# Reordering the output-projection stage of a one-core hybrid encoder layer: variance before half a weight remainder, three row blocks of one column half first, MLP turns earlier

## The reference, cut to what matters

```
u = rms_norm(h, g_pre_mix)
proj = u @ w_in                                   # 1024 x 2304
o_a, o_b, o_c = stick_breaking(...), rg_lru(...) * gelu(...), sliding_window(...)
mixed = concat(rms_norm(o_a, ga), rms_norm(o_b, gb), rms_norm(o_c, gc))
y = mixed @ w_out                                 # 1024 x 1024
h = h + rms_norm(y, g_post_mix)
u = rms_norm(h, g_pre_mlp)
f = square(relu(u @ w_ff_in))                     # 1024 x 4096
h = h + rms_norm(f @ w_ff_out, g_post_mlp)
```

## Time and profile before

| | |
|---|---|
| median of 3 runs | 1014.74 us (1014.56 to 1014.86) |
| profiled execution, its own time | 1013.88 us |
| profiled execution, span | 1012.0 us |
| PE busy | 999.9 us (99% of the span) |
| DVE busy | 778.8 us (77%) |
| ACT busy | 577.4 us (57%) |
| POOL busy | 79.2 us (8%) |
| granted TensorE clock, mean | 0.999 |

### The profile page before, as it was taken

How to read it: one execution, slowest core, us unless ns; L and a number is a source line. 1 busy time by engine, 2 the same in 40 slices (tenths; PEclk the granted TensorE clock), 3 DMA queues, 4 the chain that set the end, 5 groups by cost and what they waited for, 6 DMA issues and landing times.

```text
span 1012.0 us, 12128 instructions
## 1 busy us (share of the span) xinstructions
PE 999.9 (99%) x4826; PEld 809.1 (80%) x4826; DVE 778.8 (77%) x723; ACT 577.4 (57%) x755; POOL 79.2 (8%) x66
## 2 busy tenths in 40 slices
PE   9999999999999999999999999999999999999997
PEld 7878778887777787888888888888888888888885
DVE  6237759898796688887777777887777887777997
ACT  7434643776886448768544656333657333647356
POOL 0013213002222231000000000000000000000000
PEclk9999999999999999999999999999999999999999
DMA  9511111200101743031031031031031031035004
GB/s 337 166 55 42 42 42 42 77 8 1 42 2 42 271 152 119 1 125 42 1 125 42 1 125 43 1 124 42 1 125 42 1 125 42 1 125 208 1 1 166
DMA packets 38864, 74.64 MB, mean 74 GB/s; under 512 B 3444, under 2 KB 12952, under 8 KB 38808
## 3 DMA queue, kind: packets, MB, share of 16 engines
q1 hardware_dynamic: 38664, 73.83, 21.3%
q10 hardware_dynamic: 144, 0.03, 0.0%
HBM read 65.46 MB, written 8.39 MB: 73 GB/s over the span
## 4 chain that ended last, share of the span: by engine, by line
PE 64%; DVE 1%; issue 0%; ACT 0%
PE ps L751 21%; PE ps L755 21%; PE ps L753 21%; PE ps L1080 1%; PE ps L1163 1%; DVE y L2082 0%; DVE y L2108 0%; DVE var L1791 0%; DVE a_op L2139 0%; DVE b_op L2150 0%; ACT y L1736 0%; DVE rs_t L1765 0%; DVE rstd L1768 0%; DVE rs_t L1767 0%; ACT ln_var L1210 0%
## 5 line engine op out<-in xcount | busy, mean ns | idle before, releaser
L751 PE MATMUL ps<-a_op,b_op 128*128 128x512 f32 x448 | 175.4, 392 | 1.1 <-DVE a_op L2139 0.6
L755 PE MATMUL ps<-a_op,b_op 128*128 128x512 f32 x448 | 174.4, 389 | 0.0
L753 PE MATMUL ps<-a_op,b_op 128*128 128x512 f32 x448 | 174.3, 389 | 0.0
L751 PE MATMUL ps<-b_op,a_op 128*128 128x512 f32 x448 | 174.3, 389 | 0.0
L753 PE MATMUL ps<-b_op,a_op 128*128 128x512 f32 x448 | 174.3, 389 | 0.0
L755 PE MATMUL ps<-b_op,a_op 128*128 128x512 f32 x448 | 174.3, 389 | 0.0
L1564 ACT CAST a_op<-f 128x1024 fp32r<-128x1024 f32 x56 | 58.7, 1048 | 112.2 <-PE ps L755 82.5
L2150 DVE TENSOR_TENSOR b_op<-wq,b_op 128x1024 fp32r<-128x1024 f32 x96 | 116.9, 1218 | 0.0
L751 PE MATMUL ps<-act_hi,w_hi 128*128 128x512 f32 x288 | 113.4, 394 | 0.4 <-DVE act_lo L1809 0.4
L755 PE MATMUL ps<-act_hi,w_lo 128*128 128x512 f32 x288 | 112.1, 389 | 0.0
L753 PE MATMUL ps<-act_lo,w_hi 128*128 128x512 f32 x288 | 112.1, 389 | 0.0
(11 more groups left out here) (230 smaller groups left out, 1625.5 us busy)
## 6 DMA issues: line engine op xcount, KB each, us to landing
wq<-in_w_ff_in SPq DMA_DIRECT2D x16, 1024.0 KB, 5.4
wq<-in_w_ff_out SPq DMA_DIRECT2D x16, 1024.0 KB, 5.1
stage<-in_w_in SPq DMA_DIRECT2D x16, 512.0 KB, 4.7
y<-in_x SPq DMA_DIRECT2D x4, 1024.0 KB, 13.3
h_spill<-y SPq DMA_DIRECT2D x8, 512.0 KB, 2.7
h_back<-h_spill SPq DMA_DIRECT2D x2, 2048.0 KB, 12.1
out<-y SPq DMA_DIRECT2D x8, 512.0 KB, 3.1
stage<-in_w_out SPq DMA_DIRECT2D x6, 512.0 KB, 3.6
```

Of the source, the lines that this page charges most:

```text
L751: nc.tensor.matmul(dst, stat[0], mov[0], start=first, stop=False, skip_group_check=chained)
L753: nc.tensor.matmul(dst, stat[0], mov[1], start=False, stop=False, skip_group_check=chained)
L755: return nc.tensor.matmul(dst, stat[1], mov[0], start=False, stop=last, skip_group_check=chained)
```

## The change

It reorders four engines' lists and gives the `a_op` slots another order. No arithmetic is added or removed.

- `OUT_ORDER` begins with row blocks 0, 1 and 2 of the left half, then 0, 1 and 2 of the right half (before: 0 and 1 of each). From step 5 on, the order is as before.
- DVE: of the last two weight remainders (L1753) only the first comes ahead of `turned_variance(2)`; then the first half-sum (n = 16), `group_rsqrt(2)`, half-sum n = 17, the second remainder, and step 1. `mix_tiles(0)` comes after step 5 (before: 4); `mix_tiles(1)` and `mix_tiles(2)` stay behind steps 8 and 12.
- PE: turns 0 to 3 come behind step 12 (before: step 14).
- ACT: turns 0 to 3 and the rounding of operand a come ahead of operand b's; the second operands (0, 1) are rounded ahead of the last row block's squares, each with a wait that the weights or rows whose memory the slot takes have been used (`y_ready` at `Y0 - 2` and `Y0 - 1`, that is 46 and 47); turn 4 is copied ahead of `scaled(6)`.
- DVE: `rest_a(0, 0)` follows directly on `rest_b(0, 0)` behind step 13; `rest_b(0, 1)` comes ahead of the last half-sum and `rest_a(0, 1)` behind `gained_last()`, ahead of `mix_tiles(3)`.

```diff
-        OUT_ORDER = ((0, 2), (1, 2), (0, 3), (1, 3)) + tuple((s, g) for s in range(2, TOK)
-                                                             for g in (2, 3))
+        OUT_ORDER = ((0, 2), (1, 2), (2, 2), (0, 3), (1, 3), (2, 3)) + tuple(
+            (s, g) for s in range(3, TOK) for g in (2, 3))
+        def a_slot(half):
+            return a_op[:, (2 - half) % A_SLOTS]
+        def b_slot(half):
+            return b_op[:, (half + 3) % B_SLOTS]
...
-                if e == len(OUT_ORDER) - 2:
+                if e == len(OUT_ORDER) - 4:
                     turn_hidden_inputs((0, 1, 2, 3))
...
-                a, b = a_op[:, (half + 2) % A_SLOTS], b_op[:, (half + 3) % B_SLOTS]
+                a, b = a_slot(half), b_slot(half)
...
             mix_squares(5)
             mix_root(2)
+            turned((0, 1))
+            round_a(0, 0)
+            turned((2, 3))
             act.wait_ge(h_ready, 6)
             round_b(0, 0)
             mix_squares(6)
-            turned((0, 1))
-            round_a(0, 0)
-            turned((2, 3))
+            act.wait_ge(y_ready, Y0 - 2)
+            round_b(0, 1)
+            act.wait_ge(y_ready, Y0 - 1)
+            round_a(0, 1)
             mix_squares(7)
             mix_root(3)
             scaled(4)
             scaled(5)
-            round_operands(0, [1])
+            turned((4,))
             scaled(6)
-            turned((4,))
             scaled(7)
...
-            split_lo(N_IN + 3, (N_IN + 3) % 2)
+            rest_weights(N_IN + 3, 0, (N_IN + 3) % 2)
+            turned_variance(2)
...
-                    if e == 0 and grp == 2:
-                        turned_variance(2)
-                        group_rsqrt(2)
...
-            mix_rows(0)
-            for j in range(3):
-                for e in range(4 * j + 1, 4 * j + 5):
+            mix_rows(0, (1,))
+            group_rsqrt(2)
+            mix_rows(0, (2,))
+            rest_weights(N_IN + 3, 1, (N_IN + 3) % 2)
+            for j, es in enumerate((range(1, 6), range(6, 9), range(9, 13))):
+                for e in es:
                     mix_rows(e)
                 mix_tiles(j)
             mix_rows(13)
             rest_b(0, 0)
+            rest_a(0, 0)
             mix_rows(14)
             mix_rows(15, (1,))
-            rest_a(0, 0)
+            rest_b(0, 1)
             mix_rows(15, (2,))
             gained_last()
+            rest_a(0, 1)
             mix_tiles(3)
-            rest_operands(0, [1])
             turned((5, 7))
```

More of the change, by code:

```diff
@@ L1563, in round_a @@
                     half_read(act, half - A_SLOTS)
-                nc.scalar.copy(a_op[:, (half + 2) % A_SLOTS, 0], src).then_inc(a_hi_ready, 1)
+                nc.scalar.copy(a_slot(half)[:, 0], src).then_inc(a_hi_ready, 1)
             def round_b(n, kk):
@@ L1571, in round_b @@
                     half_read(act, half - B_SLOTS)
-                nc.scalar.copy(b_op[:, (half + 3) % B_SLOTS, 0], src).then_inc(b_hi_ready, 1)
+                nc.scalar.copy(b_slot(half)[:, 0], src).then_inc(b_hi_ready, 1)
             def round_operands(n, kks=range(2)):
@@ L2136, in rest_a @@
                 half = 2 * n + kk
-                slot = a_op[:, (half + 2) % A_SLOTS]
+                slot = a_slot(half)
                 dve.wait_ge(a_hi_ready, half + 1)
@@ L2145, in rest_b @@
                 half = 2 * n + kk
-                slot = b_op[:, (half + 3) % B_SLOTS]
+                slot = b_slot(half)
                 src = {P1: wq11, P2: wq21, P6: wq11, P5: w_sum, P7: wq12, P3: wq22,
```

## The result

The changed kernel takes 1017.11 us (median of 14 runs) against 1014.77 for the kernel before (14 runs): ratio 1.0025, 95% interval 1.0018 to 1.0032. It is slower by 2.3 us; 1016.8 was forecast. (Two of the 14 runs took 1019.1 and 1019.4, which nothing here explains; the median does not rest on them.)

What follows compares the result with a forecast made beforehand. PE was taken as the bound, busy 999.9 of 1012.0 us, with 3.2 us of stalls to win. Terms +1.5, -1.85, -0.6, +0.8 - 0.3, +0.7, -1.5, -0.8 made 2.0 us slower: 1016.8 us, range 1012.1 to 1018.0.

Steps and rivals of the forecast that it cites:

- both collisions: POOL's gains of row blocks 2 and 6 each hold up DVE instructions with two SBUF inputs; chance 0.68, 1016.8 us.
- Variance ahead of half the remainder: Half-sums 21 and 22 on PE: the 1.7 us stall goes, a stall of 0.2 stays; gain 1.5 us.
- fourth rival: DVE's unexplained 0.45 us ahead of the reductions comes back fully: 0.35 more on any case; half chance taken.
- Three row blocks first, and `mix_tiles(0)` behind step 5: POOL's gain of row block 2 delays `mix_tiles(0)` on DVE; half-sum 32 starts at 360.9, loss 1.85 us.
- The next pair: `mix_tiles(1)` begins late through ACT's chain; half-sum 38, due at 369.1, starts at 369.7: loss 0.6 us.
- the first collision: POOL's gain of row block 2 beside `mix_tiles(0)` on DVE, making L2082 wait; half-sum 32 loses 1.85 us.
- Remainders together: `rest_a(0, 0)` directly behind `rest_b(0, 0)` on DVE: loss 0.3 us at product 0 (0.8 before), 1.5 at turn 4.
- The step that named POOL as next in turn: POOL's gain of row block 6 goes between the two remainders; `rest_a(0, 0)` ends 1.08 us after POOL.
- Turn 8: PE's turn 8, due at 395.6, waits for `scaled(7)`, done at 396.3: loss 0.8 us.
- Only the second collision: Rival: `scalar_tensor_tensor` runs beside POOL at row block 2, only row block 6's gain collides; 1014.3 us, chance 0.17.
- only the first: Rival: only row block 2's gain collides; DVE's second remainder wins over POOL, or POOL comes later; 1014.5 us, chance 0.08.
- no collision: Rival: POOL's gains of row blocks 2 and 6 cost DVE under 0.3 us each; 1012.1 us, chance 0.07.

Runs made afterwards that it cites:

- gain2_waits: The changed kernel, but POOL begins the gain of row block 2 only when both h of `mix_tiles(0)` are written: 1014.87 us.
- gain2_under_h: The changed kernel, but POOL begins the gain of row block 2 when the Newton steps of `mix_tiles(0)` are done: 1016.27 us in one run.
- variance_alone: The kernel before with only the variance ahead of the second remainder; `OUT_ORDER` and the place of `mix_tiles(0)` stay: 1016.97 us.
- gain6_waits: The changed kernel, but POOL begins the gain of row block 6 only when the remainder of the first operand a is written: 1014.68 us.
- turns_alone: The kernel before with only the MLP part: turns 0 to 3 behind step 12, ACT's and DVE's operands as in the change: 1015.49 us.
- both_wait: The changed kernel with POOL's gains of row blocks 2 and 6 both made to wait: 1012.45 us.

## Why the prediction was right, point by point

The forecast named both collisions, their place and what each would cost PE. Every term came out within 0.25 us. A stall costs PE some 0.08 more behind it than the late start itself, since the second matmul then follows the first by 0.31 instead of 0.23 (361.94 and 362.25); this is called the restart below.

- *Variance ahead of half the remainder*: +1.5 forecast, 1.25 measured. Half-sum 21 has no wait and half-sum 22 starts 1.35 us earlier than before (346.91 to 345.56); with the restart behind it, half-sum 23 starts 1.25 earlier. The term was sized 0.25 too well: DVE stood 0.29 with no releaser ahead of half-sum 16's take-out, which delays half-sum 20 by 0.12 and half-sum 22 by 0.22. The gap stands at this place, with 0.27 to 0.29, in all seven traces with this order, and ahead of the reductions, with 0.44 to 0.46, in the three with the old one, so it is no accident of one execution. That it is one gap that has moved, the prediction's fourth rival, is likely but not shown; what causes it stays open.
- *Three row blocks first, and `mix_tiles(0)` behind step 5*: loss 1.85 forecast for half-sum 32. It lost 1.7 (due 360.2 in after's time, started 361.94) and 0.1 more by the restart behind it. The mechanism, POOL holding a Newton step for its whole 2.4 us, is seen in the row at 355.83, and removed by gain2_waits. In the changed kernel only the Newton step met POOL; that L2082 would have waited too is seen in gain2_under_h. That the order itself costs nothing is seen in gain2_waits too; that it is needed is seen in variance_alone.
- *The next pair*: loss 0.6 forecast, 0.54 measured (0.38 idle and the overlap of 0.16); DVE waited 0.81 for ACT's root, as the chain over the store and `scaled(1)` said. Without the first collision 0.1 to 0.2 was forecast, and gain2_waits loses 0.16. `mix_tiles(2)` met the gain of row block 5 for 0.07 (forecast: less than 0.1).
- *Remainders together*: loss 0.3 at product 0, and 1.5 at turn 4. Measured: idle 0.17 and 1.22, from start to start 0.3 and 1.4. Cause shown by gain6_waits. The step that named POOL as next in turn rested on one pair; it is now seen in the changed kernel, in gain2_waits, in turns_alone and in gain2_under_h.
- *Turn 8*: 0.8 forecast, 0.7 measured (0.57 and the overlap).
- *The rivals.* "Only the second collision" was priced at 1014.3, gain2_waits gives 1014.87; "only the first" at 1014.5, gain6_waits gives 1014.68; "no collision" at 1012.1, both_wait gives 1012.45. All three are 0.2 to 0.6 higher, the 0.25 of the first term being part of each.

What was thin in it: that a `scalar_tensor_tensor` waits for POOL's whole instruction was read from 0.03 us of L1920, a number that the prediction itself gave to either side. The mechanism was named with a chance of 0.68 and not known; the runs above are what shows it.

The Trainium skill, GPSIMD Engine Reference, section 1, names contention with DVE instructions in a 2-port mode or with two SBUF inputs. The runs agree for two SBUF inputs, in `tensor_tensor` (3.43 us) and `scalar_tensor_tensor` (2.39 us alone, 4.62 us as a pair), and for L2115 with its PSUM input they show none; that the loss is a whole instruction of the other engine is this case's measurement.

## What to carry to other kernels

When an order is changed, look not only at who waits for the result but at which instruction of the engine that shares its memory access will start in that microsecond: here a 0.16 us step took 2.4, and no view of waits shows it, only a duration above the usual one of its form. An engine that has nothing urgent to do (POOL here, 8% busy) is worth holding back by a wait until the urgent pair on the other engine is through: two such waits turned 2.3 us slower into 2.3 us faster. In this kernel the take-outs from PSUM were a safe place to have POOL at work (0.74 or 0.75 us each and POOL 2.40 to 2.42, together as alone); back-to-back instructions with two SBUF inputs were not, since POOL went in between them.

The view of waits is blind to short losses too: a start that is late by 0.16 to 0.25 had no row here. Compare starts with the pace.

## What the runs showed of the hardware that was not expected

- A tiny instruction is held as long as a large one: 2 elements per partition waited 2.2 us for POOL's 1024 (the row at 355.83; in gain6_waits the same step takes 2.39 us again).
- In variance_alone's profiled execution the granted clock fell from 2.4 to 1.2 GHz for 3.5 us (347.2 to 350.7) after PE had been idle for 2.24. PE had idle times of 1.57 in the changed kernel and 1.56 before, without a fall. The fall cost 1.6 us, beside 2.24 for the wait itself. That the idle time brought it about fits the order of events and is not shown by a run that changes it alone.

One more row goes beyond the two SBUF inputs. The variance of `mix_tiles(2)`, a `tensor_scalar` with one input, in SBUF, is dispatched while POOL still runs and takes 0.23 us instead of 0.16, ending 0.03 after POOL:
```profile
374.98 2.40 POOL L747 TENSOR_TENSOR y_gained<-y,rs_row 128x1024 f32<-128x1024 f32 x1 [1.00 <-DVE y L2115]
...
377.18 0.23 DVE L1783 TENSOR_SCALAR var<-sumsq 128x2 f32<-128x2 f32 x1
```
It takes 0.20 to 0.23 in all six traces where it meets POOL's end, and 0.16 in the four where it does not. So it seems to be held as well. The longest such hold here is 0.07, and what it would lose to a whole POOL instruction is not shown.
